# Expert biases of a mixture-of-experts block: seeded into PSUM from copied rows instead of by selector products

## What is computed

```python
def expert_rows(args):
    xe, e = args
    hh = xe @ w1[e] + b1[e]                 # 1024 -> 2048
    glu = jnp.minimum(hh[:, :D_FF], SWIGLU_LIMIT)
    lin = jnp.clip(hh[:, D_FF:], -SWIGLU_LIMIT, SWIGLU_LIMIT)
    act = glu * jax.nn.sigmoid(SWIGLU_ALPHA * glu) * (lin + 1.0)
    return act @ w2[e] + b2[e]              # 1024 -> 1024
```

## Time and profile before

| | |
|---|---|
| median of 3 runs | 1466.24 us (1465.7 to 1467.75) |
| the profiled execution | 1467.1 us, its span 1465.2 us |
| TensorE busy | 1432.4 us (98% of the span) |
| DVE busy | 1306.8 us (89%) |
| ACT busy | 1100.8 us (75%) |
| moved by DMA | 451.31 MB, mean 308 GB/s |

### The profile page before, as it was taken

One profiled execution on the slowest core, in us unless ns is written; L12 is line 12 of the kernel. 1 busy time (PEld: TensorE's weight loads), 2 busy tenths in 40 slices (PEclk: granted clock), 3 DMA queues, 4 the chain that ended last, 5 costly groups with the idle time before them and its releaser, 6 DMA issues.

```text
span 1465.2 us, 22341 instructions
## 1 busy us (share of the span) xinstructions
PE 1432.4 (98%) x7069; PEld 1165.2 (80%) x7069; DVE 1306.8 (89%) x1520; ACT 1100.8 (75%) x1345; POOL 381.0 (26%) x178
## 2 busy tenths in 40 slices
PE   9999999989999999999999999999999999999995
PEld 7777787777888888888888888888888888888884
DVE  5778765568999999999999999999999999999997
ACT  5668555357888888788888888888888888878884
POOL 3000000041333333333333333333333333333222
PEclk9999999999999999999999999999999999999998
DMA  8021022269999999999999999999999999999953
GB/s 260 16 72 58 29 87 77 112 214 391 407 395 393 393 385 389 386 383 384 371 372 386 371 377 386 370 377 381 371 380 377 376 376 375 374 382 380 366 219 126
DMA packets 98058, 451.31 MB, mean 308 GB/s; under 512 B 11427, under 2 KB 23715, under 8 KB 65250
## 3 DMA queue, kind: packets, MB, share of 16 engines
q1 hardware_dynamic: 90706, 434.16, 77.0%
q0 software_dynamic: 7312, 16.63, 5.0%
HBM read 440.46 MB, written 18.48 MB: 313 GB/s over the span
## 4 chain that ended last, share of the span: by engine, by line
PE 86%; DVE 7%; ACT 3%; DMA 2%; issue 1%; POOL 0%; SPq 0%; ACTq 0%; POOLq 0%; DVEq 0%
PE zpair L2206 47%; PE bank L2206 24%; PE bank L1906 2%; PE bank L1794 2%; PE bank L1796 2%; PE bank L1795 2%; PE bank L2156 2%; PE bank L2164 1%; DVE stage_lo L1217 1%; DVE lbuf L1297 1%; PE zpair L2175 1%; DMA x_scratch<-qk,sidx 1%; DVE pt_lo L1306 1%; DMA tn_scratch<-qk 1%; DVE lbuf L1293 0%
## 5 line engine op out<-in xcount | busy, mean ns | idle before, releaser
L1217 DVE TENSOR_TENSOR stage_lo<-ring,stage_hi 128x1024 fp32r<-128x1024 f32 x796 | 946.1, 1219 | 42.2 <-ACT stage_hi L793 13.8
L793 ACT CAST stage_hi<-ring 128x1024 fp32r<-128x1024 f32 x796 | 828.0, 1054 | 172.6 <-PE zpair L2206 141.6
L2206 PE MATMUL zpair<-stage_hi,act_hi 128*128 128x512 f32 x1024 | 322.6, 396 | 0.3 <-DVE act_lo L1610 0.3
L670 POOL COPY sidx<-gtab 96x1 int32 (+1 forms) x31 | 230.3, 7428 | 350.4 <-ACT qk L1103 350.4
L2206 PE MATMUL zpair<-stage_hi,act_lo 128*128 128x512 f32 x1024 | 316.6, 390 | 0.0
L2206 PE MATMUL zpair<-stage_lo,act_hi 128*128 128x512 f32 x1024 | 316.2, 390 | 0.3 <-DVE stage_lo L1217 0.2
L2206 PEld LDWEIGHTS zpair<-stage_lo,act_hi 128*128 128x128 f32 x1024 | 192.0, 188 | 42.3 <-DVE stage_lo L1217 1.1
L2206 PEld LDWEIGHTS zpair<-stage_hi,act_lo 128*128 128x128 f32 x1024 | 192.2, 188 | 41.1
L2206 PEld LDWEIGHTS zpair<-stage_hi,act_hi 128*128 128x128 f32 x1024 | 187.2, 188 | 43.8 <-issue 7.9
L2206 PE MATMUL bank<-stage_hi,act_hi 128*128 128x512 f32 x512 | 161.1, 396 | 0.0
L2206 PE MATMUL bank<-stage_hi,act_lo 128*128 128x512 f32 x512 | 158.1, 390 | 0.0
(11 more groups left out here) (296 smaller groups left out, 1422.2 us busy)
## 6 DMA issues: line engine op xcount, KB each, us to landing
ring<-in_w SPq DMA_DIRECT2D x384, 1024.0 KB, 8.2
ring<-in_w_in SPq DMA_DIRECT2D x12, 1024.0 KB, 5.3
ring<-in_w_out SPq DMA_DIRECT2D x4, 1024.0 KB, 4.8
xs_all<-in_x SPq DMA_DIRECT2D x4, 512.0 KB, 5.3
ring<-in_x SPq DMA_DIRECT2D x4, 512.0 KB, 3.7
tn_scratch<-qk SPq DMA_DIRECT2D x4, 512.0 KB, 3.5
x_scratch<-ring SPq DMA_DIRECT2D x4, 512.0 KB, 3.8
ring<-x_scratch SPq DMA_DIRECT2D x4, 512.0 KB, 6.0
```

The costliest lines, as they stand in the source:

```text
L670: nc.gpsimd.tensor_copy(sidx[:], gtab[:, i:i + 1] if isinstance(i, int) else gtab[:, bass.ds(i, 1)]).then_inc(sidx_copied, 1)
L793: nc.scalar.copy(dst, src).then_inc(split_hi, 1)
L1217: nc.vector.tensor_tensor(dst, src, hi_ap.bitcast(F32), ALU.subtract).then_inc(split_lo, 1)
L2206: mm = pe.matmul(bank[b0 + h][:], w[:, k, :], m[:, j % STAGES, h * BANK:(h + 1) * BANK], start=start and w is T_hi and m is stage_hi, stop ...
```

## The change

1. **Copies in DRAM.** A new DRAM tensor `b1_scratch` of 32 x 96 x 2048 holds each expert's bias 96 times, once for each token row. Twelve transfers of 2 MB (`copy_b1`) write it, in three groups of four between the loads of the attention's weights: ahead of w_in load 7, of load 10, and of w_out load 1.
2. **A load for each item.** `load_b1(e, i)` brings the item's 96 x 2048 values in two halves into `b1b`, which lies in parts of the activation buffers that are free in this stage. In the loop it is issued after the second weight load. There is one buffer; a load waits until the item before has been seeded.
3. **Seeds.** ACT copies the halves into the PSUM pairs (`seed`), the glu half for item t+1 after piece 20 of body t and the lin half after piece 22. TensorE's first product of a half waits for its seed and accumulates on it. So that it accumulates, each bank is written once at the start by a small product (`arm`), in the place of some of the filler products (`keep_busy`).
4. **Gone:** the selector products and their waits, `select1` on DVE, the loads, the copy and the subtraction that made `bias1`, and the small tables for the selectors.

```diff
+            def copy_b1(r0, n):
+                for r in range(r0, r0 + n, 8):
+                    sp.dma_start(b1_d[:, r:r + 8, :], b1[0].unsqueeze(1).to_broadcast([E, 8, 2 * D])).then_inc(b1_copied, 16)
             for n in range(W_IN_LOADS):
+                if n in (7, 10):
+                    copy_b1(0 if n == 7 else 32, 32)
...
             for m in range(W_OUT_LOADS):
+                if m == 1:
+                    copy_b1(64, 32)
...
-            sp.wait_ge(split_lo, W_IN_PIECES + 8)
-            for g in range(4):
-                for r in (32 * g, 32 * g + 16):
-                    sp.dma_start(b1raw[r:r + 16, :].rearrange("p (h n) -> p h n", h=2),
-                                 b1[0][:, g * BANK:(g + 1) * BANK].rearrange("(h e) n -> e h n", h=2)).then_inc(bias_in, 16)
+            def load_b1(e, i):
+                wait(sp, b1_set, 2 * i)
+                if isinstance(i, int) and i == 0:
+                    sp.wait_ge(b1_copied, 16 * CAP // 8)
+                for h in range(2):
+                    half = slice(h * D, (h + 1) * D)
+                    src = b1_d[e, :, half] if isinstance(e, int) else b1_d[bass.ds(e, 1), :, half].rearrange("e r n -> r (e n)")
+                    sp.dma_start(b1b[h][0:CAP, :], src).then_inc(b1_in, 16)
...
                     for c in (4, 5):
                         load_w1(0, c, moe_slot(c))
+                    load_b1(0, 0)
                 sp.wait_ge(tn_ready, t + 1)
                 sp.dma_start(tn_d[t * P:(t + 1) * P, :], tn[t]).then_inc(tn_out if t else tn_first, 16)
...
             with sp.Fori(2, E) as t:
                 for c in range(SLOTS):
                     load_body(t, t - 1, c, MAIN.freed(t - 1, c))
+                    if c == 1:
+                        load_b1(t, t)
...
+            def seed(i, h):
+                act.wait_ge(b1_in, i * 32 + 32)
+                nc.scalar.copy(zpair[h][0:CAP], b1b[h][0:CAP, :].rearrange("p (b n) -> p b n", b=2)).then_inc(b1_set, 1)
...
                         if j == 19:
                             gate(t)
+                        if j == 20 and not last:
+                            seed(t + 1, 0)
                         if j == 21 and not last:
                             x_evac(t + 1)
+                        if j == 22 and not last:
+                            act.wait_ge(clipped, t * 2 + 2)
+                            seed(t + 1, 1)
...
-            def bias_1(t, halves):
-                pe.wait_ge(sel1_r, t + 1)
-                wait(pe, clipped, t * 2)
-                for h in halves:
-                    for c in range(4):
-                        r = slice(32 * c, 32 * c + 32)
-                        sel = sel1b if h and len(halves) > 1 else sel1
-                        mm = pe.matmul(bank[c][:], sel[r, :], bias1[r, h * BANK:(h + 1) * BANK], start=h == halves[0], stop=False)
-                mm.then_inc(sel1_used, 1)
+            def arm(b):
+                for h in range(2):
+                    mm = pe.matmul(bank[b][:, 2 * P * h:2 * P * (h + 1)], identB[:], masks[:], start=h == 0, stop=h == 1)
+                return mm
...
-                        bias_1(t, halves)
                     pe.wait_ge(xT_lo_r, t * 2 + (1 if first else 2))
                     for j in range(W1P):
+                        if j < 2:
+                            pe.wait_ge(b1_set, t * 2 + j + 1)
```

More of the change, by code:

```diff
@@ L249, in build @@
         over_hit = slot(11)[:, 0:16 * WIDE].rearrange("p (a e) -> p a e", e=WIDE)
-        b1raw = slot(9)[:, 0:D]
+        b1b = [over("b1_glu", [P, D], F32, act_at + 4 * 2 * D), over("b1_lin", [P, D], F32, act_at + 4 * (KT * S + 2 * D))]
         b2raw = over("b2raw", [P, D], F32, act_at + 4 * (KT * S + 3 * D))
@@ L1089, in a_evac, with seed_first @@
                     nc.scalar.copy(aT_hi[:, 4 * h:4 * h + 4, 0:CAP], bank[6 + h][:, 0:4 * CAP].rearrange("p (k t) -> p k t", k=4)).then_inc(aT_hi_r, 1)
+            def seed(i, h):
+                act.wait_ge(b1_in, i * 32 + 32)
+                nc.scalar.copy(zpair[h][0:CAP], b1b[h][0:CAP, :].rearrange("p (b n) -> p b n", b=2)).then_inc(b1_set, 1)
+            def seed_first():
+                act.wait_ge(armed, 1)
+                act.wait_ge(b1_in, 32)
+                for b in range(2):
+                    ins = nc.scalar.copy(bank[4 + b][0:CAP, :], b1b[0][0:CAP, b * BANK:(b + 1) * BANK])
+                ins.then_inc(b1_set, 1)
+                seed(0, 1)
             def gate(t):
@@ L1113, in turns @@
                     return 16 * (loads_before(z) + k)
+                if b == MOE0:
+                    seed_first()
+                else:
+                    seed(q0, 0)
+                    seed(q0, 1)
                 for j in range(W1P):
@@ L1126, in run_items @@
                 if b == MOE0:
+                    act.wait_ge(armed, 2)
+                    seed(q0 + 1, 0)
                     x_next(q0 + 1, 0, None)
@@ L1137, in body @@
                             if b == MOE0:
+                                act.wait_ge(clipped, 1)
+                                seed(q0 + 1, 1)
                                 x_next(q0 + 1, 1, ub + W1P)
@@ L1701, in body @@
                             weights(t - 1)
-                        if j == 7 and not last:
-                            select1(t + 1, both)
                         if j == 12:
@@ L2211, in run_items @@
                 q0, n, b, T0 = run.first, run.n, run.base, run.turn0
-                low, high = ((0,), (1,)) if run is MAIN else ((0, 1), (0, 1))
                 if b == MOE0:
-                    pe.wait_ge(bias_lo, 2)
-                    pe.wait_ge(sel1_r, 1)
-                    bias_quarters((4, 5, 2, 3), range(4))
+                    for z in (4, 5, 2):
+                        arm(z)
+                    arm(3).then_inc(armed, 1)
                     pe.wait_ge(tables, 1)
@@ L2219, in run_items @@
                     weight_table((0, 1))
-                    keep_busy(0, 3)
+                    keep_busy(0, 1)
+                    arm(0)
                     pe.wait_ge(counts_read, 1)
-                else:
-                    bias_1(q0, low)
                 turn_x(q0)
@@ L2226, in run_items @@
                     weight_table((2,))
-                    keep_busy(0, 6)
+                    for _ in range(3):
+                        arm(0)
                 pe.wait_ge(xT_lo_r, 2 * q0 + 1)
                 for j in range(W1P):
+                    if j < 2:
+                        pe.wait_ge(b1_set, 2 * q0 + j + 1)
                     if j == W2P:
@@ L2266, in body @@
                             turn_a(t)
-                body(1, low, first=True)
-                if run is MAIN:
-                    with pe.Fori(2, 16) as r:
-                        body(r, low)
-                with pe.Fori(16 if run is MAIN else 2, n - 1) as r:
-                    body(r, high)
-                body(n - 1, high, last=True)
+                body(1, first=True)
+                with pe.Fori(2, n - 1) as r:
+                    body(r)
+                body(n - 1, last=True)
                 pe.wait_ge(aT_lo_r, 2 * (q0 + n) - 1)
```

68 lines of the change are left out of this document (21 added, 47 removed).

## The result

The changed kernel takes 1618.64 us (median of 4 runs, 1617.75 to 1637.75); the kernel before took 1466.62 us on the same chip. The ratio is 1.1066, 95% interval 1.1038 to 1.1093: slower by 152 us, where 21.5 us was forecast and the range ended at 1504.

A forecast was written before the change was run, and what follows sets the result against it. TensorE, busy 98%, was taken as the bound, with DVE and transfers close behind. Transfers would then set the pace: 26 items at +0.78 us (+20.3), last item -0.8, start +2, together +21.5: about 1488 us, range 1460 to 1504.

The forecast's parts named there:

- what the change adds to the transfers: Expert stage: 0.786 MB more an item, 13.86 MB at 390 GB/s, 35.55 us instead of 34.77; chance 0.47.
- 96 rows are dearer than their bytes: Rival, item bias loads: 96 rows count as 128, 36.2 us an item, +39 us, 1505 us; chance 0.10.
- Engines: Expert stage: selector products gone save 0.53 us, seeds delaying DVE take back 0.5 us; 34.75 us an item.
- The 0.10 us ahead of the selector products: TensorE at a body's start: part of the 0.53 us that may be the loop's branch and stay.
- Place and order: Expert stage: ACT's seed waits for the bias landing from about the sixth item, TensorE idle there; landings stay at 20 us.
- The 23.6: Expert stage: us the bias load may take from its issue at about 705.3 until ACT's first seed at 728.97.
- The start: Start of the expert stage: first item's bias queues ahead of the last token store, delaying the gather; +2 us.
- The copies: Attention: bias copies written in DRAM are hidden, 0 us; rival that they hold the loads, +5 to +15 us, chance 0.04.
- The gain stays: Rival, expert stage: over 399 GB/s and seeds DVE does not feel, -10 us, 1456 us; chance 0.16.

The follow-up runs named there:

- e2: The changed kernel with 128 bias copies in DRAM and item loads of all 128 rows instead of 96: 1513.65 us, ratio 1.0323.
- e8: The changed kernel without bias loads and seeds for items 2 to 31, so their values are wrong: 1449.8 us, ratio 0.9887.
- e1: The changed kernel without the bias loads of items 2 to 31, whose seeds copy item 1's bias: 1470.42 us, ratio 1.0024.
- e4: The changed kernel without copies in DRAM; each load reads the expert's one row of b1 96 times: 1625.75 us, ratio 1.1088.
- f1: The kernel before plus unread loads an item into rows 0-63, each half in eight transfers of every eighth row: 1633.61 us, ratio 1.1137.
- e6: The kernel before plus two unread loads an item into rows 0-63, 0.52 MB: 1628.75 us, ratio 1.1108.
- e7: The kernel before plus two unread loads an item into rows 32-95, 0.52 MB: 1465.76 us, ratio 0.9996.
- e10: The kernel before plus two unread loads an item, one half into rows 0-95, the other into 32-127: 1609.16 us, ratio 1.0968.
- g2: The kernel before plus unread loads into rows 32-95, each half cut in two transfers at partition 64: 1582.23 us, ratio 1.0794.

## Why the prediction was wrong

**The step that failed** is in what the change adds to the transfers: "At 390 GB/s that takes 35.55 us". The bytes were right (13.8 MB an item). The capacity was taken as a property of the core and its mix of bytes, 390 GB/s, and was read from a stage in which every large transfer fills 128 rows. The added transfer of 96 rows pulled it down to 347 GB/s, so the item takes 39.9 us: 5.1 us over before, not 0.78. With 128 rows the term would have held: e2 moves 389 GB/s. Why a short transfer slows the others is not shown.

**The rival that came nearest** was that 96 rows are dearer than their bytes. Its direction was right and its size was not: it counted them as 128 rows, 36.2 us an item and 1505 us. That is what 128 rows cost when they are really loaded (36.23 us, 1513.65). The 96 rows cost 105 us more. A bound that counts a short transfer as a full one is no upper bound: it assumed that the added transfer hurts only itself, and it slowed the twelve weight loads around it. The rule of the Trainium skill on ports, which the rival named, was the right place to look, but there it prices one transfer; for a transfer amid others at capacity only runs could tell.

**Engines.** Right in the mechanism: seeds of 0.95 us, DVE late behind them, and an item of 34.75 us with seeds and no loads, as forecast. That the number fits to the hundredth is luck, since both parts were larger than summed and cancel: the selector products 0.68 instead of 0.53, the seeds 0.66 instead of 0.5. The 0.10 us ahead of the selector products, which could have been the loop's, was theirs: in e8 the pairs on both sides of the loop's end begin 0.46 us apart (732.73 and 733.19).

**Place and order.** The wait is where it was put, ACT's seed on the bias landing, with TensorE idle behind it; landings stay above 20 us. But it begins with item 2, the third, and not about the sixth. ACT there:

```profile
385.94 1.01 ACT L1111 COPY zpair<-b_glu 96x1024 f32<-96x1024 f32 x1 [1.89 <-DMA b_lin<-b_scratch]
```

The load of this item took 20.80 us from 365.11, as long as forecast (20). What failed is the room: ACT stood ready at 384.05, 18.9 us after the issue and not 23.6. The 23.6 was read from an item at 700 us, where the queue had long drained.

**The start.** The last token store takes 11.70 us to land instead of 8.21, +3.5 instead of +2; it is issued 1.3 us earlier, so it lands 2.2 us later than before. In e1 it is issued as late as before (310.76 us) and takes 11.50. e1, whose items take no longer than before, is 3.9 us slower, and its first gate after 400 us is as much later (417.9 for 414.0): the start, of which this landing is 3.3 us.

**The copies.** Hidden, as taken: the last token store is issued at 309.55 us, at 310.86 before. e4, without copies, is no faster.

**The gain stays** fell in e1: without the loads of items 2 to 31 the change is still 3.9 us slower. The note of the Trainium skill in ScalarE: Activation LUTs, that ScalarE writes PSUM faster than SBUF, shows no gain here: 1.01 us and 0.95 us to the next for 96x1024 into PSUM, 1.05 and 0.94 for the cast of 128x1024 in SBUF.

No version that adds every item's bias beats the kernel before. The best of the changed ones is e2. e8, which leaves the bias out, gains 17 us; by its items some 21 us is the most that another way to add this bias could win in the expert stage.

## What to carry to other kernels

Where the DMA engines are near their capacity, price an added transfer by what it does to the others, not by its bytes: look at which partitions one transfer writes, and make it even on both sides of partition 64 in one transfer (all 128 rows, or 32 to 95, the two forms that ran here), even if that means more bytes. Do not cut it into many small transfers for this: f1's gap costs as much. A share of 1.0 with fewer GB/s than before is the mark of it. And a capacity read from a stage holds for the shapes of that stage; add the new shape to the kernel before, with nothing that reads it, and look at the rate before building the rest.

## What the runs showed of the hardware

- Beside a stream of 1 MB loads of 128 rows at 376 to 399 GB/s, 0.52 MB an item in two transfers of rows 0-63 lowers the total to 335 GB/s; rows 64-127 to 354; rows 32-95 leave it at 390. That is 4% of the bytes, and the time rises by 11%. The loss is the others' too: e6's items move 0.52 MB more than before's and take 5.6 us longer, in which 390 GB/s would move 2.2 MB.
- The other transfers' packets take longer: w1's packets of 8192 bytes 366 ns on the mean in e6, 321 in e7 (900 to 1100 us).
- It does not even out over transfers issued next to each other (e10, g2). The Trainium skill tells in DMA: Bandwidth & Descriptors, under Back-pressure in remote DMA, that a saturated port of SBUF holds back the engines that send to it. That would fit, but it speaks of another kind of transfer, and the trace has neither ports nor the engine of a packet; so why one transfer's evenness counts, and not the sum of neighbours, stays open.
- One core sustains 389 to 402 GB/s from DRAM for whole items (e2, e7), above the 358 GB/s that the Trainium skill gives for a core's HBM limit in DMA: Bandwidth & Descriptors, under Specifications; by its own division, 716 GB/s by two cores, that is a half share, and here one core ran.
- After the 4.46 us without a product that end at 705.51, TensorE ran at the lower of its two levels (1.2 of 2.4 GHz): the granted clock from 705.5 to 711 us is 0.52. Pairs that else begin 0.45 us apart begin 0.83 to 1.02 us apart up to 710.78. The window, then TensorE in order of time:

```profile
705.50:711.00 5.50, 5.49 (x13) 4.33 (x14) 5.20 (x6) 5.46 (x8) 0.00 (x0) 0.52 1.02 407
```

```profile
700.44 0.61 PE L2217 MATMUL bank<-stage_lo,act_hi 128*128 128x512 f32 x2
705.51 1.22 PE L2217 MATMUL bank<-stage_hi,act_hi 128*128 128x512 f32 x2 [4.46 <-ACT stage_hi L813]
706.53 1.05 PE L2217 MATMUL bank<-stage_hi,act_lo 128*128 128x512 f32 x2
...
710.78 0.63 PE L2217 MATMUL bank<-stage_hi,act_hi 128*128 128x512 f32 x2
711.25 0.62 PE L2217 MATMUL bank<-stage_hi,act_lo 128*128 128x512 f32 x2
```

From 900 to 1100 us the granted clock is 0.93, against 0.98 in e6, which takes 10 us more; so the clock is not what makes the changed kernel slow.
